# A depthwise convolution moved from four engines to TensorE alone, with DMA-shifted copies of its input

## The reference, cut to what matters

```python
def conv_module(h, w_pw1, w_dw, b_dw, ln_g, ln_b, w_pw2):
    u = h @ w_pw1                       # 1024 -> 2048
    a, gate = jnp.split(u, 2, axis=-1)
    u = a * jax.nn.sigmoid(gate)
    u = depthwise convolution, 31 taps, padding 15 on both sides, one filter per channel, + b_dw
    u = jax.nn.silu(layer_norm(u, ln_g, ln_b))
    return u @ w_pw2                    # 1024 -> 1024
```

## Time and profile before

| | us |
|---|---|
| median of 3 runs | 1775.43 |
| lowest and highest of them | 1774.36, 1779.6 |
| profiled execution: span from first to last instruction | 1782.4 |
| PE busy in it | 1549.7 |
| DVE busy | 954.1 |
| ACT busy | 629.2 |
| POOL busy | 698.5 |

### The profile page before, as it was taken

The page is one execution under the profiler, slowest core; times in us unless marked ns, Lnnn a source line. Parts: engine busy times, 40 slices in busy tenths (PEclk is TensorE's granted clock), DMA queues, the critical chain, the costliest instruction groups (busy, mean ns, idle before and its releaser), DMA issues.

```text
span 1782.4 us, 22938 instructions
## 1 busy us (share of the span) xinstructions
PE 1549.7 (87%) x9538; PEld 1281.0 (72%) x9538; DVE 954.1 (54%) x1012; ACT 629.2 (35%) x771; POOL 698.5 (39%) x609
## 2 busy tenths in 40 slices
PE   5697789888999987877659699999997779979999
PEld 5575578888999985752217488888885654579999
DVE  7875665455544456999975622222224566453443
ACT  4221115334334452445422322232222325534443
POOL 5999982201002402669602233343330530014553
PEclk8898889998999998998868899999999978989999
DMA  6553547543565542324423033222222220035552
GB/s 235 189 177 112 185 142 241 191 134 106 187 188 181 177 140 86 106 80 167 179 87 132 26 116 95 94 95 94 95 94 71 71 94 1 1 95 180 179 186 95
DMA packets 147452, 227.36 MB, mean 128 GB/s; under 512 B 4353, under 2 KB 119201, under 8 KB 147105
## 3 DMA queue, kind: packets, MB, share of 16 engines
q1 hardware_dynamic: 147024, 225.53, 38.1%
q10 hardware_dynamic: 336, 0.55, 0.1%
HBM read 225.01 MB, written 1.05 MB: 127 GB/s over the span
## 4 chain that ended last, share of the span: by engine, by line
PE 64%; DVE 19%; POOL 13%; issue 2%; ACT 1%; DMA 1%; POOLq 0%; DVEq 0%; ACTq 0%
PE bank L1670 18%; PE bank L1671 18%; PE bank L1672 18%; DVE A L1366 9%; POOL A L1564 2%; DVE A L1333 2%; POOL A L1566 2%; POOL A L1565 2%; PE bank L2054 2%; PE bank L2032 2%; POOL A L1567 2%; POOL A L1581 1%; POOL alo L483 1%; PE bank L2043 1%; POOL A L1580 1%
## 5 line engine op out<-in xcount | busy, mean ns | idle before, releaser
L1670 PE MATMUL bank<-ahi,whi 128*128 128x256 f32 (+1 forms) x2480 | 802.0, 323 | 87.8 <-POOL alo L483 51.4
L1671 PE MATMUL bank<-alo,whi 128*128 128x256 f32 (+1 forms) x2480 | 792.5, 320 | 0.0
L1672 PE MATMUL bank<-ahi,wlo 128*128 128x256 f32 (+1 forms) x2480 | 791.3, 319 | 0.0
L977 DVE TENSOR_TENSOR wlo<-raw,whi 128x2048 fp32r<-128x2048 f32 x154 | 357.3, 2320 | 529.5 <-ACT whi L518 529.0
L518 ACT ACTIVATE whi<-raw 128x2048 fp32r<-128x2048 f32 x160 | 306.3, 1914 | 814.0 <-PE bank L1672 814.0
L1670 PEld LDWEIGHTS bank<-ahi,whi 128*128 128x128 f32 x2480 | 485.2, 196 | 138.2 <-issue 68.5
L1671 PEld LDWEIGHTS bank<-alo,whi 128*128 128x128 f32 x2480 | 485.6, 196 | 29.0 <-issue 0.7
L1672 PEld LDWEIGHTS bank<-ahi,wlo 128*128 128x128 f32 x2480 | 484.8, 195 | 29.7
L1609 POOL TENSOR_TENSOR alo<-A,ahi 128x512 fp32r<-128x512 f32 (+1 forms) x43 | 125.8, 2927 | 281.2 <-ACT ahi L693 281.2
L483 POOL TENSOR_TENSOR alo<-A,ahi 128x512 fp32r<-128x512 f32 x36 | 57.3, 1596 | 369.1 <-ACT ahi L478 369.1
L1366 DVE SCALAR_TENSOR_TENSOR A<-A 128x512 f32<-128x512 f32 (+1 forms) x145 | 159.4, 1099 | 5.0
(11 more groups left out here) (252 smaller groups left out, 1534.3 us busy)
## 6 DMA issues: line engine op xcount, KB each, us to landing
raw<-in_w_ff SPq DMA_DIRECT2D x64, 1024.0 KB, 5.4
A<-in_w_mod SPq DMA_DIRECT2D x96, 512.0 KB, 4.9
raw<-in_w_in SPq DMA_DIRECT2D x28, 1024.0 KB, 7.5
raw<-in_pw SPq DMA_DIRECT2D x12, 1024.0 KB, 5.3
raw<-in_w_ffn_gate SPq DMA_DIRECT2D x11, 1024.0 KB, 5.4
raw<-in_w_ffn_up SPq DMA_DIRECT2D x11, 1024.0 KB, 5.3
raw<-in_w_ffn_down SPq DMA_DIRECT2D x11, 1024.0 KB, 5.0
raw<-in_w_qkv SPq DMA_DIRECT2D x6, 1024.0 KB, 5.0
```

The lines of the kernel that those rows point to most:

```text
L977: dve.tensor_tensor(wlo[:, k % 2, :], raw[:, (k + 2) % 4, :], whi[:, k % 2, :].bitcast(F32), ALU.subtract).then_inc(wlo_ready, 1)
L1670: pe.matmul(out_, w_hi, a_hi, start=start, stop=False, **kw)
L1671: pe.matmul(out_, w_hi, a_lo, start=False, stop=False, **kw)
L1672: return pe.matmul(out_, w_lo, a_hi, start=False, stop=stop, **kw)
```

## The change

All eight chunks are convolved on PE. 31 taps become 8 groups of 4. Four taps by 32 channels fill the 128 rows of the array, and the products for four such sets of 32 channels go to four column tiles. The stationary matrices (128 x 32, diagonal in each block of 32 rows) are built on the host, 512 KB for each chunk, and come by DMA (`load_taps`) into a ring of four. The moving operand needs the input at four shifts on four groups of partitions. DVE writes the gated product of a pair of chunks into a staging buffer, and ACT issues 16 DMAs for each pair (`shift_copies`), each of 32 partitions by 4 rows of 284 elements (145 KB, so 2.33 MB for a pair), from SBUF to SBUF. ACT copies each finished chunk with its bias (`convolved`). DVE, ACT and POOL no longer compute taps.

The order on PE becomes: six blocks of `pw1`; chunk 0 and two modulation pieces, chunk 1 and two pieces; the last two blocks of `pw1`; chunks 2 to 7, each followed by its pieces (2, then 3 each) and the channel sum of the chunk two earlier. The ring of modulation pieces shrinks from six buffers to four, and SP's order of loads is written out anew.

```diff
+TAP_GROUPS = 8
+PADW = 288
+SHIFTW = 284
+MOD_IN_CONV = [2, 2, 2, 3, 3, 3, 3, 3]
...
+            def load_taps(c):
+                if c == 0:
+                    sync.wait_ge(evac["ple"], 4)
+                    sync.wait_ge(nlo_ready, 16)
+                if c >= 4:
+                    sync.wait_ge(conv_done, c - 3)
+                sync.dma_start(area(7424 + 1024 * (c % 4), 1024), I["w_dw"][c]).then_inc(taps_landed[c % 4], 16)
...
                 if name == "pw1":
-                    for l in range(8):
+                    for l in range(6):
                         load(name, Pos(FIRST[name] + l, l))
                         if l == 4:
-                            sync.wait_ge(nlo_ready, 16)
-                        if l >= 4:
-                            load_mod(1, l - 4)
-                    load_mod(1, 4)
-                    load_mod(1, 5)
+                            load_taps(0)
+                            load_taps(1)
+                            for t in range(3):
+                                load_mod(1, t)
+                    t = 3
+                    for l in range(6, 8):
+                        load_mod(1, t)
+                        load_mod(1, t + 1)
+                        t += 2
+                        load(name, Pos(FIRST[name] + l, l))
+                    for l in range(2):
+                        load("pw2", Pos(FIRST["pw2"] + l, l))
+                    for c in range(2, KD):
+                        load_taps(c)
+                        for _ in range(MOD_IN_CONV[c]):
+                            load_mod(1, t)
+                            t += 1
+                    continue
                 if name == "pw2":
-                    for t in range(6, HALVES):
+                    for l in range(2, 4):
+                        load(name, Pos(FIRST[name] + l, l))
+                    for t in range(t, HALVES):
                         load_mod(1, t)
...
+            def shift_copies(h):
+
+                act.wait_ge(u_ready, 2 * h + 2)
+                if h >= 2:
+                    act.wait_ge(conv_done, 2 * h - 2)
+                for j in range(4):
+                    for q in range(4):
+                        act.dma_start(shifted[32 * j:32 * j + 32, h % 2, q, :, :, :],
+                                      stage[32 * q:32 * q + 32, h % 2, :, :, j:j + SHIFTW])\
+                           .then_inc(shifted_landed[h % 2], 16)
+
+            def convolved(c):
+                act.wait_ge(conv_done, c + 1)
+                act.activation(cacc[:, c, :, :], pb[4 + c % 2][:, :].rearrange("p (s t) -> p s t", s=2), ACT.Identity,
                                bias=C["convb"][:, c:c + 1]).then_inc(conv_out, 1)
...
             def act_pw1(p):
+                h = p.least // 2
+                if p.least == 7:
+                    convolved(0)
+                    convolved(1)
                 ahead(p)
                 if p.least % 2:
                     act.wait_ge(block_done, p.b + 1)
...
+                    shift_copies(h)
 
             each_block(act, "pw1", act_pw1, roll=False)
             mod_rows(1, 0)
-            for i in range(len(CONV_PE) * TAPS):
-                diagonal(i)
-                products(None, 1)
...
+            for c in range(2, KD):
+                convolved(c)
+                if c == 4:
+                    mod_rows(1, 1)
+            mod_rows(1, 2)
...
+            def pw1_block(l):
+                p = Pos(FIRST["pw1"] + l, l)
+                if l >= 4:
+                    pe.wait_ge(u_ready, 6 if l >= 6 else 2)
+                feature_block(p, KD, lambda m: pb[pw1_bank(l) + m][:, :], 0, 512,
+                              (lambda c: wait_norm(pe, 3, c)) if l == 0 else None)
+
+            def convolve(c):
+
+                r, m = c // 2 % 2, c % 2
+                pe.wait_ge(taps_landed[c % 4], 16 * (c // 4 + 1))
+                if m == 0:
+                    pe.wait_ge(shifted_landed[r], 256 * (c // 4 + 1))
+                if c == 0:
+                    pe.wait_ge(u_ready, 4)
+                if c >= 2:
+                    pe.wait_ge(conv_out, c - 1)
+                for g in range(TAP_GROUPS):
+                    for q in range(4):
+                        mm = pe.matmul(pb[4 + c % 2][32 * q:32 * q + 32, :], taps[:, c % 4, g, q, :],
+                                       shifted[:, r, q, m, :, 4 * g:4 * g + T1], start=(g == 0),
+                                       stop=(g == TAP_GROUPS - 1))
+                mm.then_inc(conv_done, 1)
...
+            for l in range(6):
+                pw1_block(l)
+            for c in range(2):
+                convolve(c)
+                mod_pieces(MOD_IN_CONV[c])
+            for l in range(6, 8):
+                pw1_block(l)
             pe.wait_ge(u_ready, KD)
...
+            for c in range(2, KD):
+                convolve(c)
+                mod_pieces(MOD_IN_CONV[c])
+                channel_sum(c - 2)
+            mod_pieces(4)
+            channel_sum(6)
+            channel_sum(7).then_inc(msum_done, 1)
+            mod_pieces(4)
             for u in range(KD):
                 pe.wait_ge(vsq_ready, u + 1)
...
             mod_pieces(HALVES)
```

More of the change, by code:

```diff
@@ L216, in program @@
         modraw_landed = [sem(f"modraw_landed{n}") for n in range(2)]
-        modraw1_landed = [sem(f"modraw1_landed{n}") for n in range(6)]
+        modraw1_landed = [sem(f"modraw1_landed{n}") for n in range(4)]
         modraw_used = sem("modraw_used")
@@ L228, in program @@
         p_landed = sem("p_landed")
-        dw_landed = sem("dw_landed")
+        taps_landed = [sem(f"taps_landed{n}") for n in range(4)]
+        shifted_landed = [sem(f"shifted_landed{n}") for n in range(2)]
         gtab_landed = sem("gtab_landed")
@@ L491, in program, with pw1_bank, half @@
         epsb = stat[:, 60:61]
+        def pw1_bank(l):
+            return 4 * (l // 2 % 2) + 2 * (l % 2) if l < 6 else 2 * (l % 2)
+        def half(bank, m):
+            return pb[bank][:, 256 * m:256 * m + 256]
         UNITS = [4, 5, 0, 1, 2, 3]
@@ L1350, in _ @@
             ph[0] = "pw1"
[L1351 to L1369, removed]
             def dve_pw1(p):
                 if p.least % 2:
+                    h = p.least // 2
+                    if p.least == 1:
+                        dve.wait_ge(pad_ready, 1)
+                    if h >= 2:
+                        dve.wait_ge(shifted_landed[h % 2], 256)
                     for m in range(2):
@@ L1902, in _ @@
             sums(pe, 3)
-            for l in range(8):
-                p = Pos(FIRST["pw1"] + l, l)
-                if l >= 4:
-                    pe.wait_ge(u_ready, 2 * ((l - 4) // 2 + 1))
-                feature_block(p, KD, lambda m: pb[2 * p.k + m][:, :], 0, 512,
-                              (lambda c: wait_norm(pe, 3, c)) if l == 0 else None)
             pieces = list(range(HALVES))
@@ L2155 @@
     wo = a["gqa_w_o_2"][0].reshape(2, 2, 4, 64, D).transpose(0, 2, 1, 3, 4).reshape(D, D)
+    w_taps = np.zeros((TAP_GROUPS * 4, D), f)
+    w_taps[:TAPS] = a["conv_w_dw_2"][0]
+    w_taps = w_taps.reshape(TAP_GROUPS, 4, KD, 4, 32)
+    tap_blocks = np.zeros((KD, 4, 32, TAP_GROUPS, 4, 32), f)
+    for ch in range(32):
+        tap_blocks[:, :, ch, :, :, ch] = w_taps[..., ch].transpose(2, 1, 0, 3)
+    tap_blocks = tap_blocks.reshape(KD, P, 1024)
     arrays = dict(
```

156 lines of the change are left out of this document (39 added, 117 removed).

## The result

The changed kernel took 1798.2 us (median of 4 runs, 1795.82 to 1804.17), the kernel before 1777.5 beside it: ratio 1.0118, interval 1.0096 to 1.014. It is slower, by 21 us. I had forecast 1781.4 and slower as the likeliest sign, with a range that ended at 1798.0. The sign and the mechanism were read rightly, the size was not: I expected 4 to 6 us.

What follows compares the result with a forecast made beforehand. DVE's taps were taken to decide the mean, at 911.8 us. `pw2`'s first block ending at 959.7 against 955.7 (+4.0), plus 2 for copies and handovers, on 1775.4 gave 1781.4 us; range 1765 to 1798, the forecast case 1775 to 1790.

Steps and rivals of the forecast that it cites:

- mean sum done: After chunk 7: pieces wait for load 24 behind `pw2`'s 2 MB, 12 us, then 5 us to 909.1, against 911.8 before.
- variance sums done: After the mean sum: 12 us again as before the change, with four more pieces in front, to 921.
- Which queue holds what: SP's and ACT's orders: block 6 idle 10 us; chunks 3, 5 to 7 wait for matrices, chunk 4 for ACT.
- The column tiles: Taps on PE: four tiles run together, 6.9 us a chunk; one by one 27.5 us, 1945 in all, chance 0.03.
- the price of the copies: Before chunk 4: 16 ACT issues of 0.44 us take 7.1 us; 2.33 MB at 401 GB/s take 5.8 us.
- The ends that I had listed: Around the forecast: loads -1 and +6, clock gaps -2 and +5, ACT's issue -1 and +3, slow copies +6.
- my 5.0 plus 0.1: Before chunks 3 and 5 to 7: a pair of 512 KB loads lands after 5.0 us, plus 0.1.
- The clock: Half clock after PE gaps of about 4 us: 2.0 us each; rival that it holds: 1767.4, chance 0.15.
- The tail: From variance sums to the end of `pw2`'s first block: 19 pieces at the loads' pace, 38.6 us, to 959.7.
- Loads ahead: Rival: SP and ACT do not hold PE, mean sum at 849, about 1720 us; chance 0.05.
- column tiles that overlap less well: Rival on the taps: 8.7 us a chunk, 14 us more in all, 1796 us; chance 0.12.
- Dear copies: Rival on `shift_copies`: issues at 0.6 to 0.7 us and copies at half rate, 1790 to 1795 us; chance 0.18.

Runs made afterwards that it cites:

- e1: Changed kernel with SP loading `pw1`'s blocks 6 and 7 before modulation loads 3 to 6: 1782.7 us, ratio 1.0041.
- e2: Changed kernel with SP issuing the tap matrices at least two chunks ahead, as far as the ring of four allows: 1769.8 us, ratio 0.9960.
- e7: Changed kernel with the loads of `pw2`'s blocks 2 and 3 (2 MB) issued behind modulation load 28: 1789.0 us, ratio 1.0061.
- e3: Changed kernel with ACT's copies out of PSUM of chunks 2 and 3 before the last 16 copy issues: 1792.4 us, ratio 1.0081.
- e8: e4 with the copies' source in DRAM (rows of `w_mod`), leaving the gated product out of the convolution: 1796.0 us, timed once.
- e9: Changed kernel with load, copy and piece orders rewritten, one-run copies, pieces among the taps, 11 left for the tail: 1729.8 us, ratio 0.9709.
- e10: As e9, but with 4, 4, 5, 5, 1, 3, 5, 5 pieces in the chunks and 16 in the tail: 1727.6 us, ratio 0.9706.
- e4: Changed kernel with each SBUF copy moving one run of 1149 elements per partition, not four rows of 284: 1795.6 us, ratio 1.0115.

## Why the prediction was wrong

By its own steps, after taking off the 2.5 us by which the profile after starts its stretch later (forecast, measured):

| step | forecast | measured |
|---|---|---|
| block 5 of `pw1` ends | 753.1 | 753.0 |
| a chunk of taps at full clock | 6.9 | 7.00, 6.87 |
| block 6 starts, after an idle stretch of | 778.7, 10 | 780.1, 11.5 |
| chunk 2 starts | 806.6 | 809.0 |
| chunk 3 starts | 821.1 | 824.1 |
| 16 issues on ACT | 7.1 | 11.9 |
| chunk 4 starts | 838.5 | 845.9 |
| chunk 7 ends | 892.1 | 904.7 |
| mean sum done | 909.1 | 922.7 |
| variance sums done | 921 | 932.0 |
| `pw2`'s first block ends | 959.7 | 973.7 |

- **Which queue holds what** was right in every place named: block 6 behind modulation loads, chunks 3 and 5 to 7 behind their matrices, chunk 4 behind ACT, the last sums behind 2 MB. e1, e2 and e7 took such waits away and got 15.5, 28.4 and 9.2 us back; e3 shortened the one before chunk 4 and got 5.8.
- **The column tiles** run side by side with weights of their own, in full: 64 instructions in 7.0 us. The speedup of 2.38 for three tiles that the Trainium skill ("TensorE: Matmul & The Clock Gate", Part 3) gives, which I had weighed as a rival at 14 us, does not show here: four took the time of one.
- **The step that failed** is the price of the copies: "A DMA issue on ACT takes 0.44 us ... 2.33 MB at 401 GB/s are 5.8 us". An issue took 0.74 us on average (11.91 by 16), where its upper end was 0.6, and the copies moved 206 GB/s. From the end of chunk 3 to the start of chunk 4 were 13.1 us where the forecast had 8.5: 4.6 of the 14 us, the largest single term. The rows I used were loads of another kind, from DRAM. e8 says that the cheaper issue alone would not have helped.
- **It was not the whole miss.** This term mended alone makes 1786, inside the range. The steps up to the start of chunk 3 add 3.0 us, chunks 4 to 7 5.2, the mean sum 1.0 and the tail 3.0, less 2.6 for the variance sums and 0.2 for chunk 3 itself: nearly every term erred to the same side. Of the 14 us, 2 stood in my sum for the copies and for handovers.
- **The range.** The ends that I had listed add up to 20 us above the forecast and 4 below, 1777 to 1801. I wrote 1775 to 1790 and gave no reason for taking less.
- **The loads** landed 0.3 to 0.6 us later than my 5.0 plus 0.1 (5.37 to 5.63), and block 7 took 7.68 us, not 6.6. The 4.4 us that I had worked out from the Trainium skill ("DMA: Bandwidth & Descriptors", Anatomy of one DMA) for a pair was further off; the page's formula is a fit for DMAs issued from GpSimd, and these are issued by SP. **The clock** cost 1.4 to 3.0 us a gap before a chunk (chunk lengths less 7.0) and 3.1 before block 6, 2.4 on average over the seven gaps, for 2.0. Chunks 4 to 7 are 5.2 us of the error with both.
- **The tail** took 41.7 us, not 38.6: the chain shows waits of 6.85, 4.70, 4.77 and 6.14 us for loads. That the pieces would keep the pace of the earlier trace rows was wrong by 3 us; the ring of four is the likely cause, but no run has a longer one. The variance sums took 9.3 us, not 12: I had written that four more pieces would warm the clock, and then taken 12 all the same. The granted clock over the sums was 0.72 before and 1.00 after, 9.88 us against 7.13.
- The stretch grew by 17.9 us. The rest, to the measured 21 us, is 2.5 us ahead of it, and what 4 runs against 4 leave open (the interval is 17 to 25 us). In the profiles of kernels with the same code up to there the stretch began anywhere from 692.3 to 701.2 us, so I take the 2.5 us for scatter; what causes it is not known.
- **The rivals.** Loads ahead (1720) was wrong for this kernel, and is nearly what e9 and e10 reach once the queues are reordered. The clock didn't hold in any gap of 3.9 us or more. The nearest number, 1796, is that of column tiles that overlap less well, and would have been luck: a chunk took 7.0 us. "Dear copies", 1790 to 1795, named the right step, but by a sum that did not happen: it counts 6 us for slow copies, while in the changed kernel ACT, not the traffic, held chunk 4, and the measured time needed the other terms as well. I gave it 0.18.

## What to carry to other kernels

Work moved to a faster engine is worth what its operands' queue allows: walk the queue of the issuing engine, and ask of every wait in it which later load it holds back, since here one load per chunk, placed behind a wait, cost 28 us. Price a transfer by rows of its own kind (source, partitions, size), and where there is none, let the range reach to twice the price in both issue and traffic. Fill gaps with work whose operands don't need the same resource at that moment: moving eleven of 48 pieces, nine of them from beside the last copies, to the tail gave 17 us.

## What the runs showed of the hardware

- A DMA issue on ACT took 0.61 us at the median with its source in SBUF (e4) and 0.44 with its source in DRAM (e8), same destination and bytes; the last 16 issues took 11.9 us with four rows per partition and 10.3 with one run.
- SBUF copies of 145 KB into 32 partitions moved 206 GB/s in four rows and 217 to 219 in one run each, with the DMA engines 98% busy or more, the same from DRAM (217 to 220), and 268 GB/s from DRAM into 128 partitions (92% busy), where loads of 512 KB and more had 346 to 401. What of this is due to size, packets or queue was not taken apart.
- Four column tiles with different weights and different moving data, 512 columns of fp32 each, ran in the time of one product: 0.86 us for four, 7.0 us for 32.
- Every idle stretch of PE of 3.9 us or more in this stretch of the changed kernel was followed by half clock (granted 0.50 from 865.2 to 870.5 us, behind a gap of 4.66), and the same 64 instructions then took 8.4 to 10.0 us.
